# Block 1's keys, values and half of its rotated queries between the pool's projections, two low parts moved to the expert stage, and the first inverse transposed by TensorE

## The chip, the cores and the metric

The kernel is one program on one core of a Trainium2 chip. It is measured by its device time in microseconds, from one launch. The core's engines run their own instruction streams and meet at semaphores: TensorE (matrix products, PE in the profile), VectorE (DVE), ScalarE (ACT), GpSimd (POOL) and SyncE (SP), which issues nearly all transfers.

## What is computed

Two blocks of a model on 512 tokens of width 1024, all in fp32. The first block has a pool mixer and an attention side by side, then a layer of 32 experts; the second a gated delta rule (linear attention in chunks) and a sparse attention side by side. Cut to what matters here:

```python
def first_block(...):
    h = rmsnorm(x, g_attn_norm)
    proj = h @ w_in
    u, q_lat, kv_lat, k_r = split(proj)               # 512, 256, 128, 32 columns
    y_pool = pool_mixer(u, w_pool, b_pool, pool_scale)
    # attention: 8 heads, 64 + 32 (rotated) of query and key, 64 of value, causal
    q = rmsnorm(q_lat, g_q_a) @ w_q_b                 # 8 x (64 + 32)
    kv = rmsnorm(kv_lat, g_kv_a) @ w_kv_b             # 8 x (64 key + 64 value)
    k_rope = apply_rope(k_r)                          # one for all heads
    ...
    x = x + concat(rmsnorm(y_pool), rmsnorm(y_attn)) @ w_out
    x = x + moe(rmsnorm(x))                           # 4 of 32 experts for each token

def gated_deltanet(...):                              # second block
    lmat = where(strict, (kb @ k.T) * decay, 0)       # for each chunk and head
    tmat = inverse(lmat + I)                          # unit lower triangular
    u, w = tmat @ vb, tmat @ (kb * exp(gc))
    ...
```

## The kernel before

The program has three stages with a barrier of all engines between them: the first block up to the routing (`first_block`), the experts (`experts`), and the second block (`second_block`). Every engine's order is written out by hand, and every dependence is a semaphore.

**Block 1.** TensorE first projects the latents (semaphore `proj_done` 1 to 4), then the pool's input `u` in four groups of 128 columns (`proj_done` 5 to 8), each of 24 products of fp32r halves (high and low parts, line 670). The halves of the input, `hT_hi`, lie in the same memory as the query tile `qT`, and the output weights `w_out` are loaded over the pool's weights; both wait for `proj_done` 8. Behind the four groups TensorE makes, in this order: four key products (line 684, `k_nope_done`), eight products for the unrotated part of the queries (line 693), four value products (line 698), and the rotated queries in two halves, each of two products of the weights (line 706) and two of the weights with swapped columns (line 708). These are fp32 products of 512 columns. ScalarE copies keys and queries to SBUF (lines 523 to 528, two copies for each product), then copies the rotated part of the key seven times to the other heads (line 531), then the values (line 535, in banks 2 and 3). VectorE makes the rotation: two products (lines 948, 949) and four sums (line 953) for each half. TensorE's scores (line 721) wait for all of this. Attention goes in 32 turns, four blocks of 128 queries with 8 heads each. In turns 2, 7, 12 and 17 TensorE also multiplies a pool group (`pool_out`, line 746) for which GpSimd has made the differences (lines 442 to 450), one group behind the other. In turn 20 the pool's norm is made by ScalarE and VectorE.

**The first expert's weights.** A chunk is 128 x 2048 of an expert's weights, loaded by SyncE into one of four ring slots; ScalarE makes its high part (`hi`, line 1387 in the expert stage) and VectorE the low one (`lo`, line 1666; in block 1 `first_lo`, line 1022). SyncE loads the next chunk into a slot when the low part of the one in it is made. Block 1 ends with the routing, in which VectorE makes all four low parts 0 to 3 of the first expert, the last two just before it reads `mod_summed`, sixteen sums of TensorE (line 848). The expert stage starts with the row list of expert 0, the gathered rows, and low parts 4 to 7. A chunk is multiplied in 12 products of 512 columns. For 30 experts the order is a loop.

**Block 2.** For each of four chunks `t` of 128 tokens VectorE makes `LT` and `AT` (lines 3072 to 3074), then the scaled queries and values. The inverse of each chunk's triangle is made by doubling: GpSimd masks `LT` to one level (`step`, line 2291), TensorE transposes it (line 2725, `joined`), and VectorE makes the first `inverse` as identity minus the transposed step, and the first `inverseT` as identity minus the step itself (line 3085). From the second level on, TensorE multiplies (`cross_of`, line 2743, and `join`), and transposes the inverse (`turn_inverse`, line 2732) for ScalarE to copy (`copy_inverseT`). The sparse attention's turns lie between these in one loop.

## Time and profile before

| what | us |
|---|---|
| median of 3 runs | 1939.27 |
| lowest and highest | 1938.44, 1946.33 |
| profiled execution, its own time | 1935.9 |
| its span | 1934.1 |

Times in the rows are microseconds from the span's start. A line of the timeline gives start, duration, engine, line and operation, the tiles written and read, the shape, and in brackets how long the engine stood idle before it and what ended that. A row with x4 merges four instructions; an fp32 product of TensorE shows as two. PE durations of single products overlap. Each line of busy time by stretch gives the stretch, its length, the busy time of PE, its weight loads, DVE, ACT and POOL, the granted TensorE clock as a share of full speed, the DMA engines' busy share, and GB/s.

### The profile page before, as it was taken

What the parts mean: (1) busy time and instruction counts of PE and PEld (TensorE: products, weight loads), DVE (VectorE), ACT (ScalarE), POOL (GpSimd) and SP (SyncE); (2) the same over time, 40 slices, a digit from 0 to 9 for tenths busy, and PEclk for the clock granted to TensorE, in tenths of its full rate; (3) what the DMA queues carried; (4) which work ended last, traced back from release to release, by engine and by line L of the source; (5) the groups of instructions that cost most, each with busy time, mean ns of one, the idle gap of its engine ahead of it and who ended that gap; (6) DMA issues with size and microseconds to landing.
All of it is one profiled execution on the core that took longest, in us unless ns stands there. A gap on an engine that the chain in (4) does not pass through costs nothing. (4 is left out here: it accounts for less than half of the span.)

```text
span 1934.1 us, 24742 instructions
## 1 busy us (share of the span) xinstructions
PE 1830.5 (95%) x8493; PEld 1404.1 (73%) x8494; DVE 1525.9 (79%) x1693; ACT 1148.5 (59%) x1218; POOL 197.6 (10%) x199
## 2 busy tenths in 40 slices
PE   6988978999999999999999999999999899998998
PEld 3546456787778777777778777778776468877985
DVE  5256666899999889999999988999998567897642
ACT  5423315677777777777777777777774644435520
POOL 0140310000000000000000000000034100104410
PEclk9988978999999999999999999999999899998999
DMA  6301836998999999999999999999997522201001
GB/s 201 104 1 45 335 124 233 359 373 351 375 380 362 371 374 348 369 381 373 359 377 377 360 356 372 363 375 382 357 373 263 162 68 88 87 23 66 2 23 44
DMA packets 103159, 499.75 MB, mean 258 GB/s; under 512 B 18737, under 2 KB 36382, under 8 KB 52834
## 3 DMA queue, kind: packets, MB, share of 16 engines
q1 hardware_dynamic: 96050, 473.37, 63.6%
q0 software_dynamic: 7056, 25.69, 3.8%
q8 instruction: 31, 0.51, 0.1%
q14 instruction: 22, 0.18, 0.0%
HBM read 478.57 MB, written 20.46 MB: 258 GB/s over the span
## 5 line engine op out<-in xcount | busy, mean ns | idle before, releaser
L1666 DVE TENSOR_TENSOR part<-ring,part 128x2048 fp32r<-128x2048 f32 x380 | 858.6, 2291 | 108.2 <-ACT part L1387 108.1
L1387 ACT ACTIVATE part<-ring 128x2048 fp32r<-128x2048 f32 x380 | 729.1, 1921 | 329.9 <-DMA ring<-in_w_gate_up 190.3
L1516 PE MATMUL bank<-part,xT_hi 128*128 128x512 f32 x2048 | 536.1, 404 | 17.8 <-DVE xT_lo L1697 13.2
L1516 PEld LDWEIGHTS bank<-part,xT_hi 128*128 128x128 f32 x2048 | 381.6, 190 | 114.3 <-issue 29.3
L1527 PE MATMUL bank<-part,actT_hi 128*128 128x512 f32 x1024 | 280.6, 396 | 1.0 <-DVE part L1666 0.7
L1516 PE MATMUL bank<-part,xT_lo 128*128 128x512 f32 x1024 | 280.8, 396 | 0.0
L1516 PEld LDWEIGHTS bank<-part,xT_lo 128*128 128x128 f32 x1024 | 194.1, 190 | 45.6
L1527 PEld LDWEIGHTS bank<-part,actT_hi 128*128 128x128 f32 x1024 | 190.2, 188 | 42.7 <-issue 1.1
L1527 PE MATMUL bank<-part,actT_lo 128*128 128x512 f32 x512 | 159.5, 393 | 0.0
L1810 POOL DMA_INDIRECT rest<-h_rows,rest x33 | 39.0, 1183 | 1115.5 <-PE bank L1499 1100.5
L1527 PEld LDWEIGHTS bank<-part,actT_lo 128*128 128x128 f32 x512 | 96.3, 188 | 21.5
L2583 PE MATMUL bank<-hT_hi,w_hi 128*128 128x512 f32 x216 | 87.0, 403 | 0.0
L2583 PE MATMUL bank<-hT_hi,w_lo 128*128 128x512 f32 x216 | 85.5, 396 | 0.0
L2583 PE MATMUL bank<-hT_lo,w_hi 128*128 128x512 f32 x216 | 84.9, 393 | 0.0
L794 PE MATMUL bank<-ring,rest 128*128 128x512 f32 x128 | 58.0, 615 | 0.0
L2583 PEld LDWEIGHTS bank<-hT_hi,w_hi 128*128 128x128 f32 x216 | 40.6, 188 | 10.2 <-issue 1.0
L2583 PEld LDWEIGHTS bank<-hT_lo,w_hi 128*128 128x128 f32 x216 | 40.6, 188 | 9.7
L794 PEld LDWEIGHTS bank<-ring,rest 128*128 128x128 f32 x128 | 25.2, 199 | 30.8 <-issue 30.8
L2583 PEld LDWEIGHTS bank<-hT_hi,w_lo 128*128 128x128 f32 x216 | 40.6, 188 | 8.9 <-issue 0.2
L553 ACT ACTIVATE rest<-bank,rest 128x128 f32<-128x128 f32 (+3 forms) x32 | 16.9, 527 | 50.6 <-DVE rest L966 50.5
L2291 POOL TENSOR_TENSOR ring<-ring,rest 128x512 f32<-128x512 f32 x28 | 33.3, 1192 | 132.1 <-DVE ring L3074 85.9
L1393 ACT ACTIVATE xT_hi<-bank 128x512 fp32r<-128x512 f32 x64 | 35.0, 607 | 19.5 <-PE bank L1499 19.5
(484 smaller groups left out, 2341.3 us busy)
## 6 DMA issues: line engine op xcount, KB each, us to landing
ring<-in_w_gate_up SPq DMA_DIRECT2D x256, 1024.0 KB, 6.6
ring<-in_w_down SPq DMA_DIRECT2D x128, 1024.0 KB, 6.9
expert_rows<-rest SPq DMA_DIRECT2D x31, 512.0 KB, 7.6
ring<-in_w_in SPq DMA_DIRECT2D x14, 1024.0 KB, 5.2
rest<-in_w_ada SPq DMA_DIRECT2D x8, 1536.0 KB, 6.6
ring<-in_w_out SPq DMA_DIRECT2D x16, 512.0 KB, 6.0
rest<-in_x SPq DMA_DIRECT2D x4, 512.0 KB, 6.6
ring<-in_w_in SPq DMA_DIRECT2D x8, 256.0 KB, 5.0
```

What stands on the lines that cost most here:

```text
L553: nc.scalar.activation(probs[:, i % 2, 0:keys(i)], bank[i % 2][:, 0:keys(i)], ACT.Exp, bias=rowmax[:, i:i + 1], scale=SCALE, accum_out=row ...
L794: ins = nc.tensor.matmul(b[:], mixT[:, k, t * P:(t + 1) * P], w_out[:, k, c * 512:(c + 1) * 512], start=(k == 0), stop=(k == KT - 1))
L1387: nc.scalar.activation(hi[part(i, c)], raw(c), ACT.Copy).then_inc(sig("hi_ready"), counts)
L1393: nc.scalar.activation(flat(xT_hi, h), bank[5 - h][:], ACT.Copy).then_inc(sig(f"xT_hi{h}"), 1)
L1516: ins = nc.tensor.matmul(bank[g][:], rows[:, c, :], w[:, g * 512:(g + 1) * 512], start=first, stop=last, skip_group_check=True)
L1527: ins = nc.tensor.matmul(bank[6 + g][:], rows[:, n, :], w[:, k, g * 512:(g + 1) * 512], start=first, stop=last, skip_group_check=True)
L1666: V.tensor_tensor(lo[part(i, c)], raw(c), hi[part(i, c)].bitcast(F32), ALU.subtract).then_inc(sig("lo_ready"), counts)
L1810: return pool.indirect_dma_start(out=f["xg"], out_offset=None, in_=m["h2_dram"], in_offset=bass.IndirectOffsetOnAxis(ap=f["index"].bitcast ...
L2291: nc.gpsimd.tensor_tensor(step_L[:, i % 2], LT[:, t], repeat(levels[:, n, :], HA), ALU.mult).then_inc(sig("step_ready"), 1)
L2583: ins = M.matmul(bank[i % 2][:], w[:, k, o], h[k // 4][:, k % 4, :], start=(k == 0 and h is hT_hi and w is w_hi[n % 2]), stop=(k == KT - 1 ...
```

## The change

It reorders three places.

1. Block 1: behind pool group 1 come keys 0, 1 and values 0, 1 (now in banks 0 and 1), behind group 2 keys 2, 3 and values 2, 3 and the first rotated half of the queries, then group 3, the second rotated half, and the unrotated queries last. ScalarE reads in that order. The seven copies of the rotated key are made by VectorE, which no longer waits for `proj_done` 8 before them, but before it writes the rotated queries. The first scores wait for two heads' unrotated queries at a time, and the first weighing for all.
2. Low parts 2 and 3 of the first expert are made in the expert stage, behind the first rows; the loads of its chunks 6 and 7 move there too, ahead of that of `b_down`.
3. Block 2: the first `inverseT` is the transpose of the first `inverse` by TensorE, copied by ScalarE, as at later levels. TensorE's first three step transposes stand ahead of its waits for all chunks, and GpSimd no longer waits for `inverseT_step`.

```diff
+FIRST = 2
 # block 1, SyncE
-            for c in range(EARLY):
+            for c in range(FIRST):
                 sp.wait_ge(sig("first_lo"), c + 1)
                 load_chunk(sp, a, m, 0, RAW + c, c)
...
 # block 1, ScalarE
+            read_u(0)
+            read_u(1)
+            for n in range(2):
+                read_k(n)
+            for t in range(2):
+                read_v(t)
+            read_u(2)
+            for n in range(2, 4):
+                read_k(n)
+            for t in range(2, T):
+                read_v(t)
+            read_u(3)
             for n in range(4):
                 act.wait_ge(sig("q_nope_done"), n + 1)
...
-            act.wait_ge(sig("k_rope_ready"), 1)
-            for h in range(1, H1):
-                ins = nc.scalar.activation(kT[64:96, h, :], kT[64:96, 0, :], ACT.Copy)
-            ins.then_inc(sig("k_rope_spread"), 1)
...
 # block 1, TensorE
+            project_u(0)
...
+            project_u(1)
             pe.wait_ge(sig("kv_norm"), 1)
             pe.wait_ge(sig("k_rope_read"), 1)
             pe.wait_ge(sig("w_kv_loaded"), 32)
+            for n in range(2):
+                make_k(n)
+            for t in range(2):
+                make_v(t)
+            project_u(2)
+            for n in range(2, 4):
+                make_k(n)
+            for t in range(2, T):
+                make_v(t)
             pe.wait_ge(sig("q_norm"), 1)
             pe.wait_ge(sig("w_q_loaded"), 64)
+            pe.wait_ge(sig("w_swap_ready"), 1)
+            pe.wait_ge(sig("var_ready"), 3)
+            make_q_rope(0)
+            project_u(3)
+            make_q_rope(1)
             for n in range(4):
...
+            pe.wait_ge(sig("uT_ready"), 4)
             pe.wait_ge(sig("q_rope_ready"), 2)
-            pe.wait_ge(sig("q_nope_ready"), 4)
...
             def scores(i):
                 q0, h = (i // H1) * P, i % H1
+                if i < H1:
+                    pe.wait_ge(sig("q_nope_ready"), h // 2 + 1)
...
             def weigh(i):
                 pe.wait_ge(sig("probsT_ready"), i + 1)
+                if i == 0:
+                    pe.wait_ge(sig("q_nope_ready"), 4)
 # block 1, VectorE
-            dve.wait_ge(sig("proj_done"), 8)
+            dve.wait_ge(sig("proj_done"), 4)
             dve.wait_ge(sig("k_rope_read"), 1)
             V.tensor_tensor(kT[64:96, 0, :], rope_c[64:96, :], rope_s[64:96, :], ALU.add).then_inc(sig("k_rope_ready"), 1)
+            dve.wait_ge(sig("k_rope_ready"), 1)
+            for h in range(1, H1):
+                ins = V.tensor_copy(kT[64:96, h, :], kT[64:96, 0, :])
+            ins.then_inc(sig("k_rope_spread"), 1)
...
                 dve.wait_ge(sig("q_rope_read"), n + 1)
+                dve.wait_ge(sig("proj_done"), 8)
                 for h in range(4):
...
-            first_lo(2)
-            first_lo(3)
             dve.wait_ge(sig("mod_summed"), 1)
 # experts, SyncE
+            sp.sem_inc(sig("y_stored"), 16)
+            for c in range(FIRST, EARLY):
+                wait_lo(sp, 0, c)
+                load_chunk(sp, a, m, 0, RAW + c, c)
             sp.dma_start(m["b_down"], a["b_down"][0]).then_inc(sig("b_down_loaded"), 16)
 # experts, VectorE
-            dve.sem_inc(sig("lo_ready"), EARLY)
+            dve.sem_inc(sig("lo_ready"), FIRST)
...
             rows_lo(1)
-            for c in range(EARLY, PARTS):
+            for c in range(FIRST, PARTS):
                 make_lo(0, c)
 # block 2, GpSimd's step
                 if 2 <= i < T + 2:
                     pool.wait_ge(sig("joined"), i - 1)
-                    pool.wait_ge(sig("inverseT_step"), i - 1)
 # block 2, ScalarE
-                act.wait_ge(sig("inverse_turned"), i - T + 1)
+                act.wait_ge(sig("inverse_turned"), i + 1)
...
+            copy_inverseT(0)
+            copy_inverseT(1)
...
-                if T <= i - 2 < 6 * T:
+                if i - 2 < 6 * T:
                     copy_inverseT(i - 2)
 # block 2, TensorE
-            pe.wait_ge(sig("chunks_ready"), T)
-            pe.wait_ge(sig("kg_ready"), T)
-            pe.wait_ge(sig("beta_v_ready"), T)
-            pe.wait_ge(sig("decay_row_ready"), T)
-            for t in range(T):
+            def turn_step(t):
+
                 pe.wait_ge(sig("step_ready"), t + 1)
+                if t == 0:
+                    pe.wait_ge(sig("LT_ready"), T - 1)
+                    pe.wait_ge(sig("decay_row_ready"), T - 1)
...
+            turn_step(0)
+            turn_step(1)
+            turn_step(2)
+            pe.wait_ge(sig("chunks_ready"), T)
+            pe.wait_ge(sig("decay_row_ready"), T)
+            turn_inverse(0)
+            turn_step(3)
+            turn_inverse(1)
+            pe.wait_ge(sig("kg_ready"), T)
+            pe.wait_ge(sig("beta_v_ready"), T)
...
-                if T <= i - 2 < 6 * T:
+                if i - 2 < 6 * T:
                     turn_inverse(i - 2)
 # block 2, VectorE
             for t in range(T):
                 one = repeat(ident, HA)
-                dve.wait_ge(sig("step_ready"), t + 1)
-                V.tensor_tensor(inverseT[:, t], one, step_L[:, t % 2], ALU.subtract).then_inc(sig("inverseT_step"), 1)
                 dve.wait_ge(sig("joined"), t + 1)
```

## Rows read from the trace of the kernel before

**Rows 1.** The page's first line.

```profile
span 1934.1 us, 24742 instructions
```

**Rows 2.** Busy time by stretch: opening, attention's start, half clock, expert loop.

```profile
79.27:114.31 35.04, 24.56 (x49) 9.45 (x47) 8.92 (x13) 16.08 (x28) 0.00 (x0) 0.87 0.42 143
114.31:144.12 29.81, 27.14 (x138) 18.76 (x139) 17.46 (x57) 11.92 (x41) 20.41 (x30) 0.86 0.00 1
156.25:170.10 13.85, 12.70 (x47) 9.07 (x46) 9.81 (x19) 2.40 (x8) 0.00 (x0) 0.51 0.01 2
330.00:1520.00 1190.00, 1171.79 (x5329) 925.10 (x5327) 1083.10 (x898) 848.30 (x691) 81.73 (x72) 1.00 0.93 362
```

**Rows 3.** Timeline of TensorE between the pool's projections and the scores.

```profile
79.27 1.88 PE L684 MATMUL bank<-rest 128*128 128x512 f32 x4
...
84.11 7.11 PE L693 MATMUL bank<-rest,ring 128*128 128x512 f32 x16 [0.18 <-ACT ring L524]
91.06 1.88 PE L698 MATMUL bank<-rest 128*128 128x512 f32 x4
96.88 3.78 PE L698 MATMUL bank<-rest 128*128 128x512 f32 x4 [3.95 <-ACT rest L535]
...
106.28 1.99 PE L706 MATMUL bank<-rest,ring 128*128 128x512 f32 x4 [1.51 <-DVE rest L949]
108.11 1.88 PE L708 MATMUL bank<-rest,ring 128*128 128x512 f32 x4
114.31 0.80 PE L721 MATMUL bank<-ring 96*128 96x128 f32 x2 [4.32 <-DVE ring L953]
```

**Rows 4.** Timeline of ScalarE and VectorE in the same stretch.

```profile
79.47 0.60 ACT L519 ACTIVATE rest<-bank 128x512 f32<-128x512 f32 x1 [4.96 <-PE bank L670]
...
92.48 3.73 ACT L531 ACTIVATE ring<-ring 32x512 f32<-32x512 f32 x7
...
111.48 2.78 DVE L953 TENSOR_TENSOR ring<-rest 32x512 f32<-32x512 f32 x4
```

**Rows 5.** Timeline of attention: TensorE's pool products and turns, and GpSimd.

```profile
117.08 2.02 PE L746 MATMUL bank<-rest,ring 128*128 128x512 f32 x2
...
123.58 1.27 POOL L450 TENSOR_TENSOR rest<-rest 128x512 f32<-128x512 f32 x1
...
143.00 1.12 PE L746 MATMUL bank<-rest,ring 128*128 128x512 f32 x2 [1.08 <-POOL rest L450]
...
155.92 0.55 PE L729 MATMUL bank<-rest 128*128 128x128 f32 x3 [2.45 <-ACT rest L553]
157.29 1.59 PE L721 MATMUL bank<-ring 96*128 96x384 f32 x2
...
170.41 1.02 PE L721 MATMUL bank<-ring 96*128 96x512 f32 x2
```

**Rows 6.** Timeline at the end of block 1.

```profile
272.69 6.96 PE L848 MATMUL bank<-rest 128*128 128x1 f32 x32
...
276.39 4.49 DVE L1022 TENSOR_TENSOR part<-ring,part 128x2048 fp32r<-128x2048 f32 x2
```

**Rows 7.** Timeline at the start of the expert stage; the page's DMA issues.

```profile
292.28 4.49 DVE L1666 TENSOR_TENSOR part<-ring,part 128x2048 fp32r<-128x2048 f32 x2 [1.11 <-ACT part L1387]
...
302.48 1.92 ACT L1387 ACTIVATE part<-ring 128x2048 fp32r<-128x2048 f32 x1 [6.91 <-PE bank L1516]
...
ring<-in_w_gate_up SPq DMA_DIRECT2D x256, 1024.0 KB, 6.6
```

**Rows 8.** Timeline of block 2 between the last chunk and the loop.

```profile
1759.97 1.19 PE L2725 MATMUL bank<-rest,ring 128*128 128x128 f32 x8 [2.52 <-ACT ring L2461]
1766.97 2.05 PE L2743 MATMUL bank<-ring 128*128 128x128 f32 x8 [1.85 <-POOL ring L2291]
...
1769.11 1.09 POOL L2291 TENSOR_TENSOR ring<-ring,rest 128x512 f32<-128x512 f32 x1 [1.33 <-PE bank L2743]
...
1772.56 1.06 PE L2743 MATMUL bank<-ring 128*128 128x128 f32 x8
```

More of the change, by code:

```diff
@@ L516, in _, with read_u, read_k @@
             rsqrt(2, inv, var)
-            for g in range(GROUPS):
+            def read_u(g):
                 act.wait_ge(sig("proj_done"), 5 + g)
                 nc.scalar.activation(uT[:, g, :], bank[2 + g % 2][:], ACT.Copy).then_inc(sig("uT_ready"), 1)
-            for n in range(4):
+            def read_k(n):
                 act.wait_ge(sig("k_nope_done"), n + 1)
@@ L658, in _, with project_u @@
             latent_sum(1, 2, bank[6][:])
-            for g in range(GROUPS):
+            def project_u(g):
                 if g < 2:
@@ L671, in _, with make_k, make_v, make_q_rope @@
                 ins.then_inc(sig("proj_done"), 1)
-                if g == 0:
-                    pe.wait_ge(sig("swap_ready"), 1)
-                    pe.wait_ge(sig("k_rope_copied"), 1)
-                    nc.tensor.matmul(bank[5][64:96, :], swap[64:96, :], k_rope[64:96, :], start=True, stop=True).then_inc(sig("k_swapped"), 1)
+            def make_k(n):
+                if n >= 2:
+                    pe.wait_ge(sig("k_nope_ready"), n - 1)
+                nc.tensor.matmul(bank[4 + n % 2][:], w_k[:, n * P:(n + 1) * P], lat[:, 0, :], start=True, stop=True).then_inc(sig("k_nope_done"), 1)
+            def make_v(t):
+                if t >= 2:
+                    pe.wait_ge(sig("v_ready"), t - 1)
+                nc.tensor.matmul(bank[t % 2][:], lat[:, 0, t * P:(t + 1) * P], w_v, start=True, stop=True).then_inc(sig("v_done"), 1)
+            def make_q_rope(n):
+                if n == 1:
+                    pe.wait_ge(sig("q_rope_read"), 1)
+                for k in range(2):
+                    nc.tensor.matmul(bank[6][:], w_qr[:, k, n * P:(n + 1) * P], lat[:, 1 + k, :], start=(k == 0), stop=(k == 1))
+                for k in range(2):
+                    ins = nc.tensor.matmul(bank[7][:], w_swap[:, k, n * P:(n + 1) * P], lat[:, 1 + k, :], start=(k == 0), stop=(k == 1))
+                ins.then_inc(sig("q_rope_done"), 1)
+            project_u(0)
+            pe.wait_ge(sig("swap_ready"), 1)
+            pe.wait_ge(sig("k_rope_copied"), 1)
+            nc.tensor.matmul(bank[5][64:96, :], swap[64:96, :], k_rope[64:96, :], start=True, stop=True).then_inc(sig("k_swapped"), 1)
+            project_u(1)
             pe.wait_ge(sig("kv_norm"), 1)
@@ L680, in _ @@
             pe.wait_ge(sig("w_kv_loaded"), 32)
-            for n in range(4):
-                if n >= 2:
-                    pe.wait_ge(sig("k_nope_ready"), n - 1)
-                nc.tensor.matmul(bank[4 + n % 2][:], w_k[:, n * P:(n + 1) * P], lat[:, 0, :], start=True, stop=True).then_inc(sig("k_nope_done"), 1)
+            for n in range(2):
[7 more added lines that the diff above has]
+                make_v(t)
             pe.wait_ge(sig("q_norm"), 1)
             pe.wait_ge(sig("w_q_loaded"), 64)
+            pe.wait_ge(sig("w_swap_ready"), 1)
[3 more added lines that the diff above has]
+            make_q_rope(1)
             for n in range(4):
@@ L694, in _ @@
                 ins.then_inc(sig("q_nope_done"), 1)
-            for t in range(T):
-                pe.wait_ge(sig("uT_ready"), 4) if t < 2 else pe.wait_ge(sig("v_ready"), t - 1)
-                nc.tensor.matmul(bank[2 + t % 2][:], lat[:, 0, t * P:(t + 1) * P], w_v, start=True, stop=True).then_inc(sig("v_done"), 1)
-            pe.wait_ge(sig("w_swap_ready"), 1)
-            pe.wait_ge(sig("var_ready"), 3)
-            for n in range(2):
-                if n == 1:
-                    pe.wait_ge(sig("q_rope_read"), 1)
-                for k in range(2):
-                    nc.tensor.matmul(bank[6][:], w_qr[:, k, n * P:(n + 1) * P], lat[:, 1 + k, :], start=(k == 0), stop=(k == 1))
-                for k in range(2):
-                    ins = nc.tensor.matmul(bank[7][:], w_swap[:, k, n * P:(n + 1) * P], lat[:, 1 + k, :], start=(k == 0), stop=(k == 1))
-                ins.then_inc(sig("q_rope_done"), 1)
+            pe.wait_ge(sig("uT_ready"), 4)
             pe.wait_ge(sig("q_rope_ready"), 2)
-            pe.wait_ge(sig("q_nope_ready"), 4)
             pe.wait_ge(sig("k_rope_spread"), 1)
```

13 lines of the change are left out of this document (7 added, 6 removed).

## The prediction

> **What bounds the kernel now.** The span is 1934.1 us [rows 1], and by stretches [rows 2] it falls into two kinds of work. In the expert loop (330 to 1520 us) TensorE is busy for 1171.8 of 1190 us at the full clock: what shifts its beginning shifts its end, and nothing of the change lies inside it. The ends are different. From 79.27 us, when the pool's four projections are over, to the first scores at 114.31 us, TensorE is busy 24.6 of 35.0 us and part of that at half clock (mean 0.87). I then followed TensorE through this stretch in order of time [rows 3]: keys from 79.27, the eight unrotated query products 84.11 to 91.22, two value products, a wait of 3.95 us for ScalarE, two value products that take 3.78 us where the first two took 1.88 (half clock), the rotated queries' two halves, the second from 106.28 and after 1.51 us of waiting, and then 4.32 us of waiting for VectorE. So this stretch is a chain of three engines with no other work on TensorE to cover it. ScalarE's part of it is seven copies of the rotated key, 3.73 us, ahead of the value copies, and VectorE's the products and sums of each rotated half [rows 4].
>
> **Part 1, block 1.** The same matrix products are issued in another order, so their sum does not change: behind 79.27 us stand 4 key and 4 value products at 1.88 us per two (7.5 us), 8 unrotated products at 7.11 us, and 2 rotated halves of 4 products each. At full clock the second half takes 108.11 + 1.88 - 106.28 = 3.71 us, two take 7.4 [rows 3]. Sum: 7.5 + 7.1 + 7.4 = 22.0 us. If TensorE never waits, its last product before the scores ends at 79.27 + 22.0 = 101.3 us.
>
> Does it wait? A pool projection lasts 4.96 + 0.60 = 5.56 us (from the copy of one to that of the next, [rows 4]). Projections 0 and 1 end at 68.1 as now; keys and values 0 and 1 by 71.9; projection 2 by 77.4; keys and values 2 and 3 by 81.2; the first rotated half by 84.9; projection 3 by 90.4; the second half by 94.1; the unrotated queries by 101.3. ScalarE's reads of two keys and two values (four copies of 0.59 and two of 0.60 us, about 3.6 us) lie under a 5.6 us projection. The second rotated half needs VectorE's two products of the first, which end at 84.9 + 1.4 = 86.3, before 94.1. The sums that write the rotated queries wait for projection 3 (their tile lies over its inputs) and take 2.77 us from 90.4; the second half's products and sums take 0.7 + 0.7 + 2.8 = 4.2 us from 94.1, so they end at 98.3, under the unrotated products. The seven rotated-key copies move to VectorE, behind the query norm near 72 us. Their form on VectorE is not in the trace; from below they cost 0, from above 0.69 us each, as the half-sized sums do, 4.9 us. VectorE has nothing else until 84.9, so either is hidden; without that cover it would cost 4.9 us. What is queued behind the new wait of the sums is only VectorE's own second half. The loads of the output weights and the biases, which wait for projection 3, begin 11 us later and need some 17 us; they are wanted when attention is over, 80 us on. So: scores at 101.4, **gain 12.9 us**. The wait for the last unrotated copy (about 102.4) now stands ahead of the first weighing, which comes later than that.
>
> **Attention's start.** Now the clock is at half when the scores begin, behind the idle time before them: the stretch to 144.12 has a mean of 0.86 [rows 2], and the first pool product takes 2.02 us where the last takes 1.12 [rows 5]. In the new order TensorE is busy without a break up to the scores, so I take full clock. The first pool product then takes 0.9 us less, and the scores ahead of it about 0.9 less. From there GpSimd's chain paces the stretch: it finishes its second difference at 123.58 + 1.27 = 124.85, and for the last one TensorE waits 1.08 us [rows 5]. So the faster clock counts only up to the first pool product, and for half a microsecond behind it: bounds 0 and 2.5, I take **1.3 us**.
>
> **Part 2, the first expert's low parts.** VectorE loses two subtractions, 4.49 us from 276.39 to 280.88 [rows 6]. But what follows them waits for sixteen sums of TensorE that end at 272.69 + 6.96 = 279.65. So VectorE goes on at about 279.75 instead of 280.85: **gain 1.1 us**, the rest turns into a wait. Behind the barrier the two subtractions come after the first expert's rows, and push low parts 4 and 5 back, from a start at 292.28 to one at 295.8 (VectorE waited 1.11 us before it); they end at 300.3. TensorE lets chunk 2 go just before 302.48 [rows 7], has chunk 3 then, and wants part 4 behind 305. The loads of the first expert's chunks 6 and 7 leave SyncE at about 293.5 and 295.8 instead of 278.7; they take about 6.6 us, until 300.1 and 302.4, and ScalarE reads them only when their targets are free, chunk 6 at 302.48 and chunk 7 one chunk of products later [rows 7]. Behind them the next expert's chunks 0 and 1 go 3.5 us later, chunks 2 and 3 as before. Cost: 0; from above, if the first comes some microseconds late, 3 us.
>
> **Part 3, the first inverse.** Now, after the last chunk, VectorE makes both the inverse and its transpose for each of four blocks [rows 8], GpSimd's second pair of steps waits for each, TensorE idles, and its clock falls: cross products begin at 1766.97, at half clock (2.05 us against 1.06). In the change the first two step transposes follow the last chunk at once (1757.5), so GpSimd starts step 2 near 1758.0 and step 3 near 1759.3; each lasts 1.09 us [rows 8], and I allow 0.2 for VectorE's work beside it. The two bias sums follow until 1762.0, step 4 until 1763.1: cross products at about 1763.1, 3.9 us earlier. TensorE gains 16 transposes, about 0.45 us per four at full clock; eight of them lie in its waiting, eight (0.9 us) inside the loop. The loop's third turn, which begins at 1772.56 now, would begin at 1763.1 + two turns (0.9 + 0.3 + 0.45 and 0.9 + 0.3 + 0.9 + 0.45 + 0.2, about 4.4) = 1767.5 at full clock, 5.1 us earlier. At half clock until about 1767 it begins at 1769.5, 3.0 us earlier. ScalarE's four added copies, 0.60 us each, lie in its idle time. The loop is full on TensorE from there, so the gain stays. I take the middle, **4.0 us**, since the new order leaves a wait of 2 us (1758.4 to 1760.4) where the present one leaves 2.52.
>
> Between 1759.97 and 1766.97 TensorE did only transposes, and the cross products behind them ran at half clock [rows 8], but the 2.52 us of idling before them may have done that. The Trainium skill (TensorE: Matmul & The Clock Gate, "Part 4: PE-mode transpose") says that transposes do not count as busy for the clock; this speaks against the change, which puts sixteen more there. By that rule part 3 gives 3.0 us, and the sum below would be 18.3 instead of 19.3; this trace does not settle it.
>
> **Sum.** 12.9 + 1.3 + 1.1 + 4.0 = 19.3 us. Against the profiled execution (1935.9 us, span 1934.1) this gives 1916.6 and a span of 1914.8; that execution stands 3.4 us under the median, so the forecast of the median is 1939.3 - 19.3 = **1920.0 us**.
>
> **The rivals.**
> *The clock does not fall at turn 21.* A wait of 2.45 us beside the pool's norm [rows 5] is followed by half clock from 156.25 to 170.1 [rows 2]; three turns take 170.41 - 157.29 = 13.1 us [rows 5], at full clock about 3.4 + 2.25 + 2.25 = 7.9. The stretch before it changes, and so may the fall: 5.2 us more, 1914.8. For it: the wait of 1.51 us at 106.28 [rows 3] was not followed by a fall at once (3.7 us of full clock behind it). Against it: nothing of the wait itself is touched.
> *Part of the opening comes back.* The clock falls between 101 and 105, where TensorE waits for the first probabilities, or ScalarE's reads delay an interleaved projection: 2 to 8 us back, about 1925. For it: the chain of the first turns is thin. Against: TensorE is full just before.
> *The opening is hidden.* Something else sets attention's pace (GpSimd's differences, the later loads of the output weights): only parts 2 and 3 stay, 5.1 us, 1934.2. Against: GpSimd's chain starts with the first scores' turn and moves with it, and the loads end 70 us early.
> *Slower.* The expert loop's transfers use 0.93 of its time [rows 2]. If the later chunks left the loop bound by them, every one of its 30 turns of 39.3 us could lose time. Slack is 0.07 x 39.3 = 2.7 us a turn, so lateness heals in two turns, unless a turn's transfers grew by more than 2.7 us. To be slower by 0.5% it takes 19.3 + 9.7 = 29 us, 0.97 us lost a turn beyond the slack: about 1949. Nothing in the rows speaks for it: the bytes are the same.
>
> **Chances.** Forecast as made 0.52 (its own range 1917 to 1923); no fall at turn 21, 0.22; part comes back 0.16; opening hidden 0.06; slower 0.04. A difference of less than 0.5%, 9.7 us, is about what a measurement cannot tell from no change. Faster by more: 0.52 + 0.22 + 0.16 = 0.90; within: 0.06; slower: 0.04. The 8 in 10 range takes in the second case and most of the third: 1911 to 1927.
>
> **What would show it.** Right: TensorE without a gap from 62 us to about 101, scores at 101.4, the key copies on VectorE done before 80; the last pool product near 130 instead of 143.00; VectorE waiting for the sixteen sums near the end of block 1; the first expert's third chunk not waited for; cross products about 5.5 us after the last chunk's end instead of 9.5. Wrong: a wait of a projection for ScalarE, scores later than 103, half clock at attention's start, a wait for chunks 6 and 7, or the first turns of the chunk loop no nearer than now.

## The result, and the profile after

The changed kernel takes 1919.1 us (median of 7 runs, 1908.8 to 1923.2) against 1939.8 (7 runs) for the kernel before: ratio 0.989, 95% interval 0.9871 to 0.9908, 17.8 to 25.0 us less. The forecast was 1920.0, with 0.90 on faster. A second series of 6 runs (e10 below) gives 0.9885 (0.9858 to 0.9912), with medians 24.4 us apart. One run of the kernel before and one of e11 fell into a slow state (3050.42 and 3036.45 us, granted clock 0.56) and stand in no median or ratio here.

The first trace of the changed kernel is of its fastest run (1908.82 us), the one of before [rows 1] of a run of 1935.9; the spans differ by 27.2 us. The page's first line:

```profile
span 1906.9 us, 24784 instructions
```

TensorE in time order, from the product that swaps the key's rows, and from the last keys to the first scores (answers to [rows 3]; start, duration, engine, line, tiles):

```profile
60.27 1.04 PE L717 MATMUL bank<-rest,ring 32*32 32x512 f32 x2
...
75.88 1.88 PE L695 MATMUL bank<-rest 128*128 128x512 f32 x4
77.60 1.88 PE L701 MATMUL bank<-rest 128*128 128x512 f32 x4
79.32 1.88 PE L708 MATMUL bank<-rest,ring 128*128 128x512 f32 x4
...
88.31 1.88 PE L708 MATMUL bank<-rest,ring 128*128 128x512 f32 x4
...
91.74 7.04 PE L744 MATMUL bank<-rest,ring 128*128 128x512 f32 x16
98.61 0.39 PE L759 MATMUL bank<-ring 96*128 96x128 f32 x2
```

The same swap in the kernel before, from which its stage lengths are counted:

```profile
61.55 1.04 PE L676 MATMUL bank<-rest,ring 32*32 32x512 f32 x2
```

No row of the changed kernel from 60.27 us to behind the first scores has a bracket: TensorE does not wait there. A unit of two fp32 products starts 1.72 us after the one before it (75.88, 77.60, 79.32), where I had counted the row's duration, 1.88. VectorE in the same time (answers to [rows 4]):

```profile
71.49 3.41 DVE L986 COPY ring<-ring 32x512 f32<-32x512 f32 x7
82.95 0.69 DVE L993 TENSOR_TENSOR rest<-bank,rest 128x512 f32<-128x512 f32 x1 [8.06 <-PE bank L710]
...
88.57 2.78 DVE L999 TENSOR_TENSOR ring<-rest 32x512 f32<-32x512 f32 x4 [4.20 <-PE bank L688]
```

The seven copies take 3.41 us and are done at 74.9, with 8.06 us of waiting behind them: hidden, as the forecast had it. The sums wait for the last pool projection; the second half's end at 96.2, 2.4 us before the scores.

Busy time by stretch (stretch, length, PE, weight loads, DVE, ACT, POOL, granted clock, DMA share, GB/s): the opening's last part, attention's start, the stretch at half clock, the end of block 1, and the start of block 2's loop. Answers to [rows 2]:

```profile
78.00:98.60 20.60, 20.60 (x60) 11.12 (x59) 8.25 (x12) 6.56 (x12) 0.00 (x0) 1.00 0.44 166
98.61:125.68 27.07, 22.77 (x136) 15.72 (x134) 17.27 (x57) 12.56 (x42) 19.69 (x28) 1.00 0.20 58
140.40:154.10 13.70, 11.35 (x41) 8.09 (x40) 9.17 (x18) 2.23 (x6) 0.00 (x0) 0.50 0.00 0
238.00:276.00 38.00, 25.17 (x117) 20.81 (x118) 22.54 (x55) 8.13 (x11) 5.08 (x9) 0.56 0.28 98
1732.00:1750.00 18.00, 14.83 (x127) 14.14 (x128) 12.89 (x31) 11.29 (x34) 11.00 (x13) 1.00 0.45 176
```

The clock is whole where it was 0.87 and 0.86, and the fall to half at turn 21 is still there. Attention's last pool product and turn 21 (answers to [rows 5]), and the ends of block 1 on TensorE and VectorE (to [rows 6]):

```profile
125.68 1.13 PE L786 MATMUL bank<-rest,ring 128*128 128x512 f32 x2 [1.09 <-POOL rest L453]
...
138.60 0.55 PE L767 MATMUL bank<-rest 128*128 128x128 f32 x3 [2.45 <-ACT rest L570]
...
143.47 1.54 PE L778 MATMUL bank<-rest 128*128 128x64 f32 x6 [2.35 <-DVE rest L1032]
...
255.88 6.41 PE L888 MATMUL bank<-rest 128*128 128x1 f32 x32
```
```profile
262.39 0.17 DVE L1141 TENSOR_TENSOR rest<-bank,rest 128x8 f32<-128x8 f32 x1 [2.85 <-PE bank L888]
...
272.69 8.89 DVE L1713 TENSOR_TENSOR part<-ring,part 128x2048 fp32r<-128x2048 f32 x4
```

VectorE now waits 2.85 us for the sixteen sums. The first expert's low parts 2 to 5 are done at 281.6; between 273 and 310 us TensorE has these three waits (answers to [rows 7]), none of them for a low part of the weights (the kernel before has the same three, of 1.62, 1.65 and 4.50 us):

```profile
273.03 3.75 PE L1563 MATMUL bank<-part,xT_hi 128*128 128x512 f32 x8 [1.62 <-DVE xT_lo L1744]
291.57 0.25 PE L1539 MATMUL bank<-rest 128*128 128x1 f16 x4 [1.65 <-DVE rest L1718]
305.65 3.78 PE L1563 MATMUL bank<-part,xT_hi 128*128 128x512 f32 x8 [4.50 <-DVE rest L1738]
```

Block 2 behind the last chunk (answers to [rows 8]): one wait of 2.69 us is left, and the loop's third turn starts at 1745.42.

```profile
1735.12 1.04 PE L2774 MATMUL bank<-rest,ring 128*128 128x128 f32 x8
1738.85 0.63 PE L2774 MATMUL bank<-rest,ring 128*128 128x128 f32 x4 [2.69 <-DVE ring L3147]
...
1740.90 1.13 PE L2794 MATMUL bank<-ring 128*128 128x128 f32 x8
...
1745.42 1.06 PE L2794 MATMUL bank<-ring 128*128 128x128 f32 x8
```

### The profile page after: what moved, and what is told of

The parts are those of the page before. It is cut to its first block and busy times, and to the rows that moved or that the text cites. A ratio compares the mean times of both kernels' runs of the same rounds, so it can differ in the third digit from the quotient of the medians.

```text
span 1906.9 us, 24784 instructions
## 1 busy us (share of the span) xinstructions
PE 1815.6 (95%) x8509; PEld 1398.2 (73%) x8510; DVE 1525.9 (80%) x1696; ACT 1146.5 (60%) x1215; POOL 201.9 (11%) x199
## 5 line engine op out<-in xcount | busy, mean ns | idle before, releaser
L1729 DVE TENSOR_SCALAR rest<-bank 128x512 f32<-128x512 f32 x64 | 41.0, 682 | 4.3 <-PE bank L1563 4.3
```

Source lines behind the costliest of these rows:

```text
L1729: V.tensor_scalar(up[:, h, :], bank[2 + h][:], LIMIT + 1.0, 1.0 - LIMIT, ALU.min, ALU.max).then_inc(sig(f"clipped{h}"), 1)
```

## The experiments

All stage lengths below are differences between rows of TensorE's timeline: the product that swaps the key's rows (60.27 us in the changed kernel), the first scores, the first expert's first product, block 2's first product, the end of the span. "Third turn" is from the last chunk's product behind the 1.23 us wait (1732.29 in the changed kernel) to the third turn of block 2's loop. All in us. The ratio is the measured one to the kernel before on the same chip, with its 95% interval. It is not the quotient of the two medians, from which it departs by up to 0.0024 (4.7 us, e8), inside the interval each time. Where an experiment has two or three theories, A, B and C are those of its expectation.

| kernel | swap to scores | scores to expert | experts | block 2 | third turn | ratio (95%) |
|---|---|---|---|---|---|---|
| before | 52.76 | 177.13 | 1231.7 | 410.9 | 18.11 | 1 |
| changed | 38.34 | 174.42 | 1227.9 | 406.0 | 13.13 | 0.9890 (0.9871, 0.9908) |
| changed, again (e10) | 38.35 | 174.67 | 1234.2 | 406.1 | 13.13 | 0.9885 (0.9858, 0.9912) |
| e1, part 1 alone | 38.34 | 175.72 | 1239.4 | 413.1 | 18.18 | 0.9919 (0.9895, 0.9943) |
| e2, part 2 alone | 52.00 | 175.71 | 1230.8 | 412.4 | 19.44 | 0.9985 (0.9968, 1.0003) |
| e3, part 3 alone | 52.01 | 176.72 | 1232.1 | 407.0 | 14.30 | 0.9973 (0.9959, 0.9987) |
| e4, part 1 not interleaved | 41.67 | 175.92 | 1232.3 | 412.9 | 18.15 | 0.9910 (0.9892, 0.9929) |
| e5, changed, clock held | 38.34 | 170.02 | 1237.3 | 405.6 | 13.13 | 0.9840 (0.9818, 0.9862) |
| e6, changed, copies on ScalarE | 43.69 | 176.42 | 1229.7 | 406.9 | 13.14 | 0.9907 (0.9887, 0.9928) |
| e7, changed, eight sums ahead | 38.34 | 170.72 | 1233.8 | 405.6 | 13.14 | 0.9876 (0.9852, 0.9899) |
| e8, clock held and sums ahead | 38.34 | 163.56 | 1231.5 | 407.4 | 14.12 | 0.9837 (0.9810, 0.9864) |
| e11, e8 again | 38.34 | 163.75 | 1233.2 | 405.5 | 13.14 | 0.9828 (0.9793, 0.9863) |
| e9, e8 and projection ahead | 38.33 | 170.03 | 1239.6 | 405.9 | 13.14 | 0.9827 (0.9795, 0.9860) |
| e12, e8 and three products ahead | 38.35 | 160.34 | 1229.0 | 405.6 | 13.14 | 0.9820 (0.9793, 0.9846) |

Read down a column, the table separates what an edit does from what varies by itself. The first column is 38.33 to 38.35 us wherever part 1 is in whole and its copies are on VectorE. The experts' column ranges from 1227.9 to 1239.6 with the loop's code the same everywhere. The changed kernel alone, traced twice, differs by 6.3 us there, so no edit can be seen to move it. Block 2 has scatter of its own: in the traces of e1, e4 and e6 the clock falls once more some 70 us before the end (0.66 from 1857.0 to 1862.0 in e1, 1.00 at the same place in the changed kernel), and from the third turn to the end they take 163.4 to 163.5 us, where the kernel before and the changed one take 161.5. Added up without the experts' column, the stages lie within the ratio's interval, but for e4 (10.3 us by the stages, 13.8 to 20.9 by the ratio) and, by under 1 us, e6 and e9.

### Each part alone (e1, e2, e3)

Part 1 alone is the diff of the first block without the two lines of `first_lo`; part 2 alone is

```diff
-            for c in range(EARLY):
+            for c in range(FIRST):
...
-            first_lo(2)
-            first_lo(3)
```

with the loads and low parts made in the expert stage; part 3 alone is the diff of the second block.

> Part 1 alone on the kernel before: keys, values and the first rotated query half between the pool's projections, the key's rotated rows copied by VectorE, and the scores' waits split by head. Theory A (the prediction's mechanism, with the sizes that the trace of the changed kernel shows): the products that stood behind the last pool projection now fill the time in which TensorE waited for the variances and the norm, so the first scores start 14 to 15 us earlier than in the kernel before once both are set against their last shared product, the last pool product comes 15 to 16 us earlier, and the whole is 13 to 17 us shorter, 1923 to 1927 against 1939.8. Rival B (much of the change's gain comes from the other parts or from the loop over the experts): this run is less than 10 us shorter.

> Part 2 alone: the low parts of chunks 2 and 3 of the first expert are made at the start of the expert stage and loaded there. Theory A: VectorE then waits for TensorE's sixteen sums, so that only about 1 us of the two low parts' 5.5 us is saved on the way to the expert stage and nothing is lost in it: 1 to 2 us shorter, within what the interval can tell. Rival B (the later loads of chunks 2, 3, 6 and 7 hold up the first expert): TensorE shows a wait for a low part in the first expert, and the run is 1 us or more longer. Rival C (the 3.4 to 3.9 us that the changed kernel gained beyond the prediction's terms come from here): 5 us shorter, seen at the first expert's second chunk.

> Part 3 alone: in the second block the first inverse is turned by TensorE, beside the steps of L. Theory A: the cross products start 5.5 to 6 us behind the last chunk's end against 9.5 before, the granted clock stays whole, and the end comes 4.5 to 5.1 us earlier. Rival B (the clock stays whole only because part 1 and 2 changed what TensorE did before): with the kernel before ahead of it, the clock falls to half at the inverse as it did there, the second cross step costs 1.2 us more, and the gain is 3.0 to 3.6.

Part 1 alone: the scores start 14.4 us earlier than in the trace of before, 13.7 earlier than in those of e2 and e3, whose openings ran 0.75 us shorter than before's. The ratio puts the whole at 15.7 us (11.0 to 20.3), the medians at 12.1, 1 us under theory A's range of 13 to 17. Theory A holds by the stages, and rival B (less than 10 us) falls. In its trace 1.4 us more are gained behind the scores (177.13 to 175.72).

Part 2 alone: VectorE's wait for the sums is there from the first, and nothing of it is lost in the experts.

```profile
278.18 0.17 DVE L1098 TENSOR_TENSOR rest<-bank,rest 128x8 f32<-128x8 f32 x1 [3.02 <-PE bank L851]
```

From the first scores to the first expert it takes 1.4 us less than before and 1.0 less than e3, which has the same code in this stage. The experts' stage is as long as elsewhere: theory A, and B and C fall. The whole is 2.9 us shorter by the ratio (-0.6 to 6.2), too little to tell from nothing by the times alone.

Part 3 alone did not decide between A and B but gave some of each: the order of A and the clock of B. Its rows behind the last chunk are those of the changed kernel, with the same wait of 2.69 us, and yet the transposes behind it run at half clock:

```profile
1755.01 1.04 PE L2727 MATMUL bank<-rest,ring 128*128 128x128 f32 x8
1758.74 1.09 PE L2727 MATMUL bank<-rest,ring 128*128 128x128 f32 x4 [2.69 <-DVE ring L3100]
...
1761.33 0.86 PE L2736 MATMUL bank<-rest,ring 128*128 128x128 f32 x4
1762.03 1.06 PE L2747 MATMUL bank<-ring 128*128 128x128 f32 x8
```

The granted clock of the stretch behind the wait, first of e3, then of the changed kernel:

```profile
1758.20:1761.80 3.60, 3.06 (x15) 3.09 (x16) 1.91 (x4) 0.60 (x1) 2.26 (x5) 0.53 0.91 305
```
```profile
1738.30:1741.90 3.60, 2.94 (x25) 2.76 (x26) 2.38 (x4) 1.20 (x2) 3.13 (x5) 1.00 0.84 313
```

The third turn comes at 14.30 us in the one and at 13.13 in the other, so the fall costs 1.2 us. In block 2 as a whole e3 gains 3.9 us, and by the ratio 5.2 (2.5 to 7.9). Of the ten traces with part 3, two (e3, e8) show the fall and eight do not; B's reason, that what goes before decides it, falls too, since e8 has part 1 and 2. The four traces without part 3 all show a fall at this place.

The rows also show how the clock rose again. In e3 it is 0.50 from 1758.5 to 1761.5 and 1.00 from 1762.0 on, and between the end of the wait at 1758.74 and the first cross product at 1762.03 TensorE did nothing but transposes; the last four of them take 0.86 us where four take 1.06 at half clock and 0.60 at the whole. In e8 it rose in the same way, between 1734.5 and 1735.0, behind the wait that ended at 1732.06.

### Is it the order or the interleaving (e4)?

```diff
+            for g in range(1, GROUPS):
+                project_u(g)
...
             for n in range(4):
                 make_k(n)
             for t in range(T):
                 make_v(t)
...
             make_q_rope(0)
             make_q_rope(1)
```

> Part 1 alone, but with nothing between the four pool projections: projections 0 to 3 follow each other as in the kernel before, then the four key products, both rotated query halves and then the rest, with the key's rotated rows still copied by VectorE and the scores' waits split. ScalarE reads in that order. (As in part 1 alone the values come before the queries.) Theory A (it is the filling of the stretch behind the projections, by order and by VectorE's copies, that counts and not the interleaving itself): TensorE's products are the same in number, so if nothing waits the scores start within 1 us of part 1 alone, 14 us earlier than in the kernel before. Theory B (the interleaving gives the readers, ScalarE and VectorE, the time to keep up): TensorE waits between the products behind the projections, for a read of banks 0, 1, 4 or 5 (0.6 to 1.0 us a read against 1.7 us a pair) and for VectorE's rotated queries, the scores start 2 to 10 us later than in part 1 alone, and the run is 4 to 12 us shorter than before.

The scores come 3.3 us later than in part 1 alone (41.67 against 38.34) and still 11.1 earlier than in the kernel before. Where the 3.3 us are:

```profile
80.05 2.35 PE L686 MATMUL bank<-rest 128*128 128x512 f32 x4 [0.43 <-ACT ring L526]
...
84.33 1.99 PE L692 MATMUL bank<-rest 128*128 128x512 f32 x4 [0.23 <-ACT rest L531]
...
91.27 1.99 PE L699 MATMUL bank<-rest,ring 128*128 128x512 f32 x4 [1.51 <-DVE rest L980]
```

From start to start these three places take 3.3 us more than units of 1.72 us would: all of it. By the scores this is theory B, near its lower end. By the whole time it is not: B put the run at 4 to 12 us under the kernel before, and the medians differ by 15.4 (1922.2 and 1937.63), more than part 1 alone's 12.1. So the 3.3 us stand on the traces alone. Most of part 1's gain at the scores is therefore not the interleaving: it is that the stretch in which TensorE waited for other engines was filled. The interleaving gives the readers (ScalarE for keys and values, VectorE for the rotated halves) a projection to work under.

### The copies of the rotated key (e6)

```diff
-            for h in range(1, H1):
-                ins = V.tensor_copy(kT[64:96, h, :], kT[64:96, 0, :])
-            ins.then_inc(sig("k_rope_spread"), 1)
...
+            for h in range(1, H1):
+                ins = nc.scalar.activation(kT[64:96, h, :], kT[64:96, 0, :], ACT.Copy)
+            ins.then_inc(sig("k_rope_spread"), 1)
```

the added lines behind ScalarE's last read of the queries.

> The changed kernel with the seven copies of the key's rotated rows back on ScalarE, behind the reads of the queries as in the kernel before; all else as changed. Theory A (the copies on VectorE are needed for the gain: the queries' last read ends at 100.0 us, seven copies at 0.53 us are 3.7 us more, and the scores wait for them): the first scores start 5 us later than in the changed kernel, measured from the product that swaps the key's rows (38.3 us there), so 43 to 44, and some 4 us of it stay at the sixteen sums. Theory B (the order of the products alone brings the gain): 38 to 40 us.

```profile
99.96 3.73 ACT L555 ACTIVATE ring<-ring 32x512 f32<-32x512 f32 x7
```
```profile
91.67 7.04 PE L748 MATMUL bank<-rest,ring 128*128 128x512 f32 x16
103.89 0.77 PE L763 MATMUL bank<-ring 96*128 96x128 f32 x2 [5.19 <-issue]
```

The scores come 5.35 us later, right behind the copies' end at 103.69 (the bracket names no releaser), and at half clock (0.77 us against 0.39). Theory A for the start of the scores: with the move of these copies to VectorE taken out 5.35 of part 1's 14.4 us are lost, with the interleaving taken out 3.3. The expectation's other half missed: it left some 4 us of the 5 at the sixteen sums, and there 6.8 are lost (202.39 us from the swap against 195.61), at the first expert 7.35. Of the 2.0 us lost behind the scores 1.3 lie ahead of the last pool product (28.36 us from the scores against 27.07), where the granted clock is 0.50 from 104 to 110 us in e6 and 1.00 in the changed kernel. The whole time shows the loss only weakly: 0.9907 (0.9887 to 0.9928) against 0.9890 and 0.9885.

### Turn 21: the rival that did not come, put in by hand (e5)

```diff
+            def fill(n):
+                pe.wait_ge(sig("pool_out"), GROUPS)
+                for _ in range(n):
+                    nc.tensor.matmul(bank[6][:], ones, w_pool.rearrange("p g n -> p (g n)"), start=True, stop=True)
...
+                if i == 22:
+                    fill(2)
                 if 1 <= i <= N_ATT:
                     turn_probs(i - 1)
+                if i == 23:
+                    fill(2)
```

> The changed kernel with four products more, which are thrown away (ones by the pool weights, 512 columns, into bank 6, free since the last pool product was read): two ahead of turning the probabilities of turn 21, in TensorE's 2.45 us of waiting there, and two ahead of weighing the values of turn 21, in the 2.35 us of the next wait. Theory A (the granted clock falls at this place because TensorE stands still in these two waits, and the fall costs what the prediction's first rival put on it): the clock stays whole between 138 and 155 us, the stretch from the first scores to the sixteen sums, 157.3 us in the changed kernel, shortens by 4 to 5.5 us. Theory B (behind the two waits other engines set the pace, so the half clock costs little): the clock stays whole and the stretch shortens by less than 2 us. Theory C (the fall comes from elsewhere): the clock falls all the same.

```profile
136.35 1.93 PE L792 MATMUL bank<-ring,rest 128*128 128x512 f32 x4
138.96 0.55 PE L767 MATMUL bank<-rest 128*128 128x128 f32 x3 [0.68 <-ACT rest L570]
...
141.05 1.88 PE L792 MATMUL bank<-ring,rest 128*128 128x512 f32 x4
143.83 0.88 PE L778 MATMUL bank<-rest 128*128 128x64 f32 x6 [0.89 <-DVE rest L1042]
```
```profile
138.00:165.00 27.00, 24.93 (x163) 18.20 (x163) 21.03 (x41) 10.45 (x28) 0.74 (x2) 1.00 0.01 1
```

The waits of 2.45 and 2.35 us are now 0.68 and 0.89, the clock stays whole for the 27 us behind, and from the first scores to the sixteen sums it takes 152.3 us instead of 157.3: 5.0 us (4.7 against the changed kernel's second trace, with 157.0), where the prediction's first rival said 5.2. Up to the first expert 4.4 are left. The median of this kernel is 30.5 us under before's. Theory A. The clock fell here in all nine traces without the four products, and in none of the five with them. In seven of the nine it fell inside the first wait or within 1.9 us behind it; in e1 and e10 it was still whole then and fell half a us behind the second wait, of 2.6 us there. Both waits were filled at once, so no run tells what filling one would do.

### The sixteen sums (e7), and both with the routing (e8, e10, e11)

```diff
+            for n in range(8):
+                ins = nc.tensor.matmul(bank[2][:, n:n + 1], acc[:, n * P:(n + 1) * P], ones[:, 0:1], start=True, stop=True, skip_group_check=True)
             pe.wait_ge(sig("first_hot"), 1)
...
-            for n in range(16):
+            for n in range(8, 16):
```

> The changed kernel with eight of the sixteen sums moved ahead of TensorE's wait for VectorE's list (3.19 us in the changed kernel, where TensorE has nothing to do); the other eight stay. Theory A (VectorE's 2.85 us of waiting for the sixteen sums is what part 2 gave back, and the sums are what is late): the wait goes, the first expert starts 2.5 to 2.9 us earlier, measured from the first scores, than the 174.4 us of the changed kernel. Theory B (another input of VectorE or of the expert stage comes just behind): less than 1 us.

VectorE's wait for the sums is gone from its timeline. The first expert comes 3.7 us earlier from the scores; 0.9 of it were there before the sums (the routing's last sums lie 152.5 us behind the scores against 153.4), so 2.8 are the sums': theory A, at its upper end. Then both, with four more discarded products at the routing:

```diff
             turn_h2(2)
+            for _ in range(2):
+                nc.tensor.matmul(bank[2][:, 0:256], ones, w_router.rearrange("p k e -> p (k e)"), start=True, stop=True)
             route(2)
             turn_h2(3)
+            for _ in range(2):
+                nc.tensor.matmul(bank[2][:, 0:256], ones, w_router.rearrange("p k e -> p (k e)"), start=True, stop=True)
             route(3)
```

> Both of these additions, the four products that are thrown away in the attention and the eight sums moved ahead, and besides two pairs of products thrown away (ones by the router's weights, 256 columns, into bank 2) in the waits ahead of the routing products of tiles 2 and 3 (1.18 and 0.69 us in the changed kernel). Theory A (the granted clock falls at the routing, for 14 us, since TensorE stands still there, and VectorE waits 3.2 and 3.0 us for products at half clock): the clock stays whole until the last routing product, which brings 2 to 4 us on top of the two others' sum, so 9 to 12 us from the first scores to the first expert against the changed kernel's 174.4, and 0.4 to 0.7% of the whole against the changed kernel. Theory B (the clock falls all the same, or VectorE's own work is what counts): no more than the two others bring.

> The changed kernel as it is, on the same chip as the two that follow, to set them against it, and for a second trace of it. Theory A (some 4 us of the 27.2 us between the first two traces are scatter of the loop over the experts, and the part of the change is 21 to 24 us): the first scores, the sixteen sums and the first expert lie at the same distances as in the first trace (38.3, 157.3 and 17.2 to 17.7 us), the loop takes anything from 1228 to 1239 us, and the median is 1916 to 1922. Rival B (the change shortens the loop too): the loop takes 1228 us again.

> The kernel with the clock held at two places and eight sums moved ahead, once more beside the changed kernel: 9 to 12 us less than it.

```profile
228.00:247.80 19.80, 16.45 (x115) 12.50 (x114) 12.71 (x30) 3.72 (x8) 3.68 (x6) 0.97 0.27 88
```

The clock is whole up to the last routing product (0.97 with the fall behind it), 10.9 us are gained up to the first expert (163.56 against 174.42), 2.8 more than e5 and e7 bring in sum (4.4 + 3.7). Side by side the changed kernel's median is 1916.39 and this one's 1904.71, 11.7 less. The changed kernel's second trace has the first's stages to 0.25 us up to the experts (174.67 against 174.42), and a loop of 1234.2 us: theory A of e10, and the shortness of the loop in the first trace was scatter.

### A projection ahead of the last turning (e9), a miss, and its cause (e12)

```diff
-            turn_mix(T - 1)
...
             project_out(0)
+            turn_mix(T - 1)
             project_out(1)
```

> The same, and the output projection of tile 0 moved ahead of the turning of the last tile's attention rows, for which TensorE waits 3.47 us with nothing to do while the projection's inputs are there. Theory A (the wait stands on the way to the end of block 1): the projections start 2 to 2.5 us earlier, the clock stays whole there, which fell for 7 us in every kernel so far, and the first expert comes 3 to 6 us earlier from the first scores than the 163.6 us of the kernel without it. Theory B (VectorE or a transfer of weights sets the pace behind it): less than 1 us.

The projection starts 3.3 us earlier (68.6 us behind the scores, 71.9 in e8), and yet the first expert comes 6.5 us later than in e8. In e9, TensorE's projection ahead of the turning and its first transposes of the normalised rows (line 851), then ScalarE's read of the turning (line 564) and its squares (line 606):

```profile
167.40 15.67 PE L842 MATMUL bank<-ring,rest 128*128 128x512 f32 x32 [1.11 <-DVE rest L1053]
...
204.39 1.97 PE L851 MATMUL bank<-rest 128*128 128x128 f32 x8 [7.15 <-DVE rest L1078]
```
```profile
183.54 0.60 ACT L564 ACTIVATE rest<-bank 128x512 f32<-128x512 f32 x1 [15.53 <-PE bank L804]
...
195.19 0.63 ACT L606 ACTIVATE rest<-rest 128x512 f32<-128x512 f32 x1 [3.07 <-DVE rest L1073]
```

The same two in e8:

```profile
170.82 0.60 ACT L564 ACTIVATE rest<-bank 128x512 f32<-128x512 f32 x1 [2.90 <-PE bank L804]
...
183.59 0.63 ACT L606 ACTIVATE rest<-rest 128x512 f32<-128x512 f32 x1 [3.07 <-DVE rest L1074]
```

The read stood at 170.82 in e8 and stands at 183.54 here. It is in ScalarE's queue ahead of the squares of x1 (line 606), which come at 195.19 instead of 183.59; GpSimd and VectorE normalise behind them, and TensorE waits 7.15 us for the result. Neither theory had named that queue. To test this, only three products go ahead:

```diff
+                        if t == 0 and c == 0 and k == 3:
+                            turn_mix(T - 1)
```

> The kernel with the clock held and eight sums ahead, and only the first three products of the output projection (tile 0, first half) moved ahead of the turning of the last tile's attention rows. They take 2.8 us at the whole clock and start at 167.4 us as in the run before, so the turning comes at 170.2 us where it came at 169.7. Theory A (the run before lost 6.3 us because the whole projection of tile 0, 14.9 us, stood ahead of the turning, whose read is in ScalarE's queue ahead of the squares that the normalisation of x1 waits for): the reads are no longer late, the projections start 2 to 2.5 us earlier, the clock stays whole there, and the first expert comes 1.5 to 4 us earlier than the 163.6 and 163.8 us from the first scores of the two traces without it. Theory B (any work ahead of the turning costs, or a transfer of weights sets the pace): no earlier, or later.

```profile
167.11 4.51 PE L844 MATMUL bank<-ring,rest 128*128 128x512 f32 x6 [1.11 <-DVE rest L1054]
171.46 0.60 PE L804 MATMUL bank<-rest 128*128 128x128 f32 x4
171.89 13.47 PE L844 MATMUL bank<-ring,rest 128*128 128x512 f32 x31
```

The squares are at 183.74, and the first expert comes 3.2 and 3.4 us earlier than in the two traces without it: theory A. The three products took 4.35 us, not 2.8: the clock fell for a while all the same (0.50 from 168 to 170), and that half of A fails. Its median is 1903.11 against 1937.12, 34.0 us less, where those of e8, e9 and e11 are 36.1 to 36.3 under the kernel before beside them. The intervals don't tell these four apart, so the 3.3 us stand on the traces alone.

## Why the prediction was right

**Behind 79.27: 22.0 us.** Measured 98.61 - 77.99 = 20.6 (77.99 is 79.27 less the 1.28 us by which this trace is ahead since its input). The difference of 1.4 is the length of the rows: four units of keys and values start 1.72 us apart instead of 1.88 (0.6), a rotated half takes 3.43 instead of 3.71 (0.6), the unrotated queries 6.87 instead of 7.11 (0.2). So the gain at the scores is 14.4 us, not 12.9: the mechanism right, the duration of a row taken for the distance between rows. Against the openings of e2 and e3, 0.75 us shorter than the one in the trace of before, it would be 13.7. That nothing waits, and that both covers (copies under 8.06 us of waiting, sums under the unrotated queries) hold, is as said.

**Attention's start: 1.3.** From the scores to the last pool product 28.69 us before [rows 5] and 27.07 after: 1.6. In e6, where the scores start at half clock in the new order, it is 28.36, so the clock is 1.3 of it. GpSimd's differences set the pace, 1.09 us of waiting for the last as before.

**Part 2: 1.1.** From the last pool product to the first expert 148.44 and 147.35: 1.1; alone 1.0 to 1.4. The rest of the 4.49 us turned into the wait of 2.85 us; e7 shows that the sums were what was late.

**Part 3: 4.0, between 3.0 and 5.1.** 18.11 - 13.13 = 5.0 at the whole clock, 3.8 where it falls. The middle was not a value that occurs. By the rule of the Trainium skill weighed there (TensorE: Matmul & The Clock Gate, "Part 4: PE-mode transpose") the added transposes would not keep the clock up and part 3 would give 3.0. Its price of 3.0 was not met. From 1735.12 to 1740.90 TensorE did transposes and waited 2.69 us, and the clock stayed at 1.00; in e3 the same rows had 0.53. What decides the fall is open, since no run here parts the transposes from the wait. For the rise the traces do not agree with the rule: in e3 and e8 the clock went from half to whole while TensorE did nothing but transposes.

**Sum: 19.3.** By the traces 14.4 + 1.6 + 1.1 + 5.0 = 22.1. The spans differ by 27.2: 1.3 more lie ahead of the change, 3.8 in the experts' loop, which scatters. The ratio says 17.8 to 25.0. The medians differ by 20.7 in the first series and by 24.4 in the second, so the forecast difference of 19.3 lies at the low end of what was measured. The sum was 2.8 too small. That the median came within 0.9 us of the forecast is in part luck.

**The rivals.** *No fall at turn 21:* did not happen; it came when the waits themselves were filled, and its price was right (5.0 for 5.2, e5). The words against it, that nothing of the wait is touched, were the right ones; with a fall in nine traces of nine, 0.22 looks too much for it. *Part of the opening comes back:* no row of it; the clock from 98.61 to 125.68 is 1.00. e6 shows what it would have taken: a wait of 5.19 us ahead of the scores. *Opening hidden:* e1 refutes it. *Slower through the expert loop's transfers:* no wait in the first expert for a low part, and e2's loop is 1230.8 us. The turn of 39.3 us in that rival's sum is too long: before, 29 turns take 1069.85 us (353.57 to 1423.42, by GpSimd's gathers), 36.9 each, and the slack would be 2.6 instead of 2.7. ScalarE waits once in the first expert for a transfer, 0.31 us:

```profile
290.44 1.91 ACT L1434 ACTIVATE part<-ring 128x2048 fp32r<-128x2048 f32 x1 [0.31 <-DMA ring<-in_w_gate_up]
```

**What stays open.** What makes the expert loop scatter by 11.7 us with the same code was not tried. Nor was what decides whether the clock falls behind the 2.69 us wait in block 2. Of the 2.0 us that e6 loses behind the scores, 1.3 were put to the half clock there by its rows, not by a run, and 0.7 were not followed. Whether the interleaving's 3.3 us and e12's 3.3 us are there in the whole time was not shown: the medians do not have them.

## What to carry to other kernels

When products are reordered to fill a wait, look in the other engines' queues too: of 14.4 us at the scores, 5.35 hung on moving seven small copies off ScalarE, and an idle TensorE filled with the wrong amount of work (e9) delayed a 0.6 us read and lost 6.5 us. Size a run of equal products by the distance between their starts, not by a row's duration. A fall of the clock behind a short wait that other engines cause can be bought off with discarded products in that wait; here four of them brought 5.0 us up to the sixteen sums, 4.4 of it up to the first expert.

## What the runs showed of the hardware

Seven copies of 32x512 fp32 from SBUF to SBUF take 3.41 us on VectorE and 3.73 on ScalarE, so 0.49 and 0.53 us each; the nearest row had bounded it by 0.69. The granted clock fell at turn 21 in all nine traces that had its wait of 2.44 or 2.45 us and the one behind it (in seven at the first wait, in two only at the second); at one of 2.69 us in block 2, with the same instructions around it, in two of ten. In those two it went back from 0.50 to 1.00 behind nothing but transposes.
